# One block of a two-block network on one core: key sums, lora's columns and the second projection's first chain in another order

## What is computed

```python
# first block: one projection for everything, of the context (256 tokens) and x (1024 tokens)
pc = modulate(rmsnorm(ctx, norm1_g), csh1, csc1) @ w_in
px = modulate(rmsnorm(x, norm1_g), sh1, sc1) @ w_in
xr, xk, xv, xw, xa, xgl = split_rwkv(px_rw, shift_mu, grid_shift(px_rw, rows))   # p + mu * (shifted - p)
kk = k * k_k
kk = kk / maximum(sqrt(sum(kk * kk, per head of 64)), 1e-12)
tw = tanh(xw)                                   # then tw @ w_up, xa @ a_up: "lora"
b_x = b_gate * dwconv3(c_gate * u, conv_w)      # short convolution over tokens
x = x + g1 * (concatenate([a_x, b_x]) @ w_out)
...
x = rmsnorm(x, final_g)
# second block
hdn = rmsnorm_2(x, norm_gain)
q_a, k_a, v_a, g_a, q_b, k_b, v_b, g_b = split(hdn @ w_in_2)
q_a, k_a, q_b, k_b = rope(rmsnorm_2(each head, its gain))
mixed = concatenate([o_a * silu(g_a), o_b * silu(g_b)])
x = x + mixed @ w_out_2
```

## Time and profile before

| | us |
|---|---|
| three runs | 2458.22, 2458.24, 2469.73 (median 2458.24) |
| the profiled execution | 2450.08 |
| its span, from first to last instruction | 2448.3 |
| PE busy in the span | 2129.4 (87%) |
| DVE busy | 1654.9 (68%) |
| ACT busy | 1268.3 (52%) |
| POOL busy | 675.0 (28%) |
| mean granted clock of PE | 0.944 of 2.4 GHz |

### The profile page before, as it was taken

One profiled execution on the slowest core, in us unless ns is written; L12 is line 12 of the kernel. 1 busy time (PEld: TensorE's weight loads), 2 busy tenths in 40 slices (PEclk: granted clock), 3 DMA queues, 4 the chain that ended last, 5 costly groups with the idle time before them and its releaser, 6 DMA issues. The chain is left out here.

```text
span 2448.3 us, 50472 instructions
## 1 busy us (share of the span) xinstructions
PE 2129.4 (87%) x21006; PEld 1686.8 (69%) x21006; DVE 1654.9 (68%) x2541; ACT 1268.3 (52%) x2327; POOL 675.0 (28%) x472
## 2 busy tenths in 40 slices
PE   5999998499999988973999999999479899778889
PEld 3777787477888743862788888887367788444567
DVE  3665555698888646236899999997367366477941
ACT  5412121476666654434788888886344443365430
POOL 0000011466666501204123322330254545000011
PEclk8999999699999998986999999999799999898999
DMA  7222233333222167326899999997353643200032
GB/s 273 65 56 72 60 83 70 79 68 68 68 69 69 42 225 267 124 113 234 292 394 385 385 388 395 389 386 266 114 190 112 203 111 95 110 1 1 1 104 78
DMA packets 163488, 398.29 MB, mean 163 GB/s; under 512 B 13231, under 2 KB 57405, under 8 KB 163261
## 3 DMA queue, kind: packets, MB, share of 16 engines
q1 hardware_dynamic: 148220, 345.23, 40.3%
q0 software_dynamic: 12224, 44.57, 6.8%
q10 hardware_dynamic: 2816, 5.26, 0.6%
HBM read 348.35 MB, written 46.66 MB: 161 GB/s over the span
## 5 line engine op out<-in xcount | busy, mean ns | idle before, releaser
L1900 DVE TENSOR_TENSOR exp_w_lo<-exp_w,exp_w_hi 128x2048 fp32r<-128x2048 f32 x186 | 414.4, 2290 | 21.9 <-ACT exp_w_hi L1857 21.7
L1857 ACT ACTIVATE exp_w_hi<-exp_w 128x1024 fp32r<-128x1024 f32 x384 | 377.3, 1052 | 66.9 <-PE bank L1819 51.7
L2091 POOL TENSOR_TENSOR w_lo<-mixT,w_hi 128x512 fp32r<-128x512 f32 (+1 forms) x112 | 153.5, 1395 | 175.7 <-ACT w_hi L2167 173.5
L1819 PE MATMUL bank<-exp_w_hi,xsT_lo 128*128 128x512 f32 x512 | 160.8, 396 | 5.7 <-DVE xsT_lo L1904 5.7
L1819 PE MATMUL bank<-exp_w_lo,xsT_hi 128*128 128x512 f32 x512 | 158.8, 392 | 0.0
L1819 PE MATMUL bank<-exp_w_hi,xsT_hi 128*128 128x512 f32 x512 | 158.5, 391 | 0.0
L1787 POOL DMA_INDIRECT moe_rows<-exp_out,idxT x16 | 25.2, 1572 | 437.8 <-DVE exp_out L1959 437.8
L2151 PE MATMUL bank<-w_hi,h_lo 128*128 128x512 f32 (+1 forms) x320 | 123.4, 386 | 1.1 <-POOL w_lo L2091 1.1
L2151 PE MATMUL bank<-w_lo,h_hi 128*128 128x512 f32 (+1 forms) x320 | 120.7, 377 | 0.0
L2151 PE MATMUL bank<-w_hi,h_hi 128*128 128x512 f32 (+1 forms) x320 | 120.3, 376 | 0.0
L1772 POOL DMA_INDIRECT xs<-xn_rows,idxT x16 | 116.0, 7250 | 14.4 <-DVE idxT L1931 5.7
(11 more groups left out here) (372 smaller groups left out, 5797.3 us busy)
## 6 DMA issues: line engine op xcount, KB each, us to landing
exp_w<-in_exp_w_gate_dram SPq DMA_DIRECT2D x64, 1024.0 KB, 9.9
exp_w<-in_exp_w_up_dram SPq DMA_DIRECT2D x64, 1024.0 KB, 10.6
exp_w<-in_exp_w_down_dram SPq DMA_DIRECT2D x64, 1024.0 KB, 7.5
mixT<-in_w_in_dram SPq DMA_DIRECT2D x96, 256.0 KB, 2.9
ada_w_second<-in_ada_w_dram SPq DMA_DIRECT2D x16, 1024.0 KB, 9.5
chunk<-rkv_scratch SPq DMA_DIRECT2D x80, 192.0 KB, 4.0
w_in_ring<-in_w_in_dram SPq DMA_DIRECT2D x26, 512.0 KB, 3.9
rkv_scratch<-work POOLq DMA_DIRECT2D x16, 640.0 KB, 5.9
```

The source lines that it names most:

```text
L1819: mm = pe.matmul(g.ps[bank + q][:, :], lhs[:, kk, :], wide[:, k, q * 512:(q + 1) * 512], start=(kk == 0 and p == 0), stop=(kk == KT - 1 an ...
L1857: last = act.activation(wh[:, n % RH, k, :], w[:, n % RING, k, :], ACT.Copy)
L1900: dve.tensor_tensor(wl[:, n % RH, :, :], w[:, n % RING, :, :], wh[:, n % RH, :, :], ALU.subtract).then_inc(lo_ok, 1)
L2091: pool.tensor_tensor(wl[:, q % SR, 0:width(q)], w[:, q % WR, 0:width(q)], wh[:, q % SR, 0:width(q)], ALU.subtract).then_inc(w_lo, 1)
```

## The change

It does five things. (1) In the first projection PE makes the head sums not behind the block of `HEADS` but inside it: two parts ahead of k-step 2, the third ahead of k-step 6; DVE takes them ahead of its weight split. (2) The `b`, `c`, `u` blocks of the fourth head move to the end of the list, and 12 comes ahead of 13; ACT does lora's `tanh` in this stage, two blocks behind; the four loads of `lora_up` are issued by SP behind the last weight load, into memory that `g2_row` uses later. (3) In both output stages DVE makes the low part of the first row tile, ahead of its weight splits. (4) In the second projection DVE makes the low part of the weight pieces 1, 3, 5 and 7 of the first block; the chains of rows 0 to 3 are written out in another order; a root of a constant stands first on ACT. (5) The norms of rows 4 to 7 come one product earlier (`START`), at m=7, 9, 19 and 21; their turns and parts stay where they are.

```diff
@@ phase_project
-    for i in range(4):
-
+    for i in range(3):
         order += [("rw", 4 + i), ("b", i), ("c", i), ("u", i)]
-    order += [("rw", j) for j in (8, 9, 10, 11, 1, 2, 3, 13, 12)]
+    order += [("rw", j) for j in (7, 8, 9, 10, 11, 1, 2, 3, 12, 13)]
+    order += [("b", 3), ("c", 3), ("u", 3)]
...
+            for d in range(2):
+                sp.dma_start(g.lora_up[0:64, d, :], g.i["w_lora_up"][0, d]).then_inc(g.up_in, 16)
+                sp.dma_start(g.lora_up[64:128, d, :], g.i["a_lora_up"][0, d]).then_inc(g.up_in, 16)
...
+                if n - 2 == order.index(("rw", 12)):
+                    act.wait_ge(mixed, n - 1)
+                    act.activation(g.lora[0:64, :], g.lora[0:64, :], ACT.Tanh)
...
+                if n in HEADS:
+                    take_key(HEADS.index(n))
                 if n + SR < NT:
                     split_lo(n + SR)
...
+            def key_sums(h, thirds):
+                pe.wait_ge(kcopied, h + 1)
+                for q in thirds:
+                    lo, hi = THIRDS[q]
+                    if 3 * h + q >= 2:
+                        pe.wait_ge(khread, 3 * h + q - 1)
+                    pe.matmul(g.ps[6 + q % 2][:, 0:hi - lo], g.c("head"), ksq[:, lo:hi],
+                              start=True, stop=True).then_inc(khead, 1)
...
+                    if n in HEADS and k in (2, 6):
+                        key_sums(HEADS.index(n), (0, 1) if k == 2 else (2,))
@@ phase_wkv
-            act.activation(g.lora[0:64, :], g.lora[0:64, :], ACT.Tanh).then_inc(tanh_ok, 1)
...
-            pe.wait_ge(up_in, 64)
-            pe.wait_ge(tanh_ok, 1)
+            pe.wait_ge(g.up_in, 64)
             pe.wait_ge(zeroed, 1)
@@ phase_mix_out (phase_second_out alike, with one subtraction)
-            for t in range(TT):
-
+            for t in range(1, TT):
                 pool.wait_ge(m_hi, t + 1)
...
+            dve.wait_ge(m_hi, 1)
+            for k, rows in ((0, g.yT), (4, g.bT)):
+                last = dve.tensor_tensor(ml[:, 0, k:k + 4, :], rows[:, :, 0:P], mh[:, 0, k:k + 4, :], ALU.subtract)
+            last.then_inc(first_lo, 1)
@@ phase_second_project
+    START = {m - 1: t for t, m in AT.items()}
...
             for q, (blk, k) in enumerate(pieces):
+                if q < KT and q % 2:
+                    continue
                 pool.wait_ge(w_hi, q + 1)
...
+            act.activation(rs[:, 0, 0:1], g.c("eps"), ACT.Sqrt).then_inc(chain_a, 1)
+            split(0)
+            root(0, 0)
+            split(1)
+            root(0, 1)
+            root(1, 0)
+            split(2)
+            high(0)
+            split(3)
+            root(1, 1)
...
-                if m in LATER:
-                    root(LATER[m], 0)
-                    root(LATER[m], 1)
+                if m in START:
+                    root(START[m], 0)
+                    root(START[m], 1)
...
             dve.wait_ge(rows_in, 32)
+            final_norm(0)
+            first_low(1)
+            second_norm(0)
+            final_norm(1)
+            first_low(3)
+            low(0)
+            second_norm(1)
...
-                if m in LATER:
-                    final_norm(LATER[m])
-                    second_norm(LATER[m])
+                if m in START:
+                    final_norm(START[m])
+                    second_norm(START[m])
```

More of the change, by code:

```diff
@@ L2627, in _ @@
         def _(dve):
+            dve.wait_ge(m_hi, 1)
+            dve.tensor_tensor(ml[:, 0, :, :], g.mixT[:, :, 0:P], mh[:, 0, :, :], ALU.subtract).then_inc(first_lo, 1)
             for k in range(KT):
```

86 lines of the change are left out of this document (44 added, 42 removed).

## The result

| | before | after |
|---|---|---|
| median of the timed runs | 2461.64 us (4 runs) | 2423.92 us (4 runs) |
| the profiled execution | 2450.08 | 2423.48 |
| its span | 2448.3 | 2421.7 |
| mean granted clock of PE | 0.944 | 0.936 |

The ratio is 0.9856, with a 95% interval of 0.9826 to 0.9887: the changed kernel is 28 to 43 us faster. The forecast was 2428.5, a gain of 29.7. Four more runs, beside 25 of the kernel before (median 2458.07), gave 0.9859 (0.9821 to 0.9896), 34.4 us between the medians.

The account below looks back on a forecast made before the run. PE was taken as the bound, busy 87% of the span, with waits caused by order. The terms sum to 29.7 us, taken off the median 2458.2 to give 2428.5; range 2414 to 2442.

Parts of the forecast that it names:

- key sums: First projection: four PE waits of 2.26 us and two clock falls of 1.55 go; gain 12.1, ends 9.0 and 12.1.
- projection's tail: End of first projection: with a u block last instead of lora, fewer closing operations on DVE and ACT; gain 1.3 us.
- recurrence's start: Earlier lora weights and tanh let PE start 3.5 us sooner, chunk loads late next; gain 3.4, ends 2.5 and 3.5.
- two output stages: DVE makes the first tile's low part, so PE starts sooner; gain 1.0 us each, ends 0 and 1.5 each.
- second projection's start: New order for rows 0 to 3 brings the last turn 2.1 us earlier; gain 2.0, ends -2 and 4.
- later rows: Second projection, rows 4 to 7: earlier norms shorten PE's waits of 13.9 us; gain 8.9, ends 5 and 13.
- four k-steps of products between: First projection: products between k=2 and k=6 let DVE take the sums, so the third finds its bank free.
- Last head's sums and the run of rw blocks: First projection: DVE falls about 7 us behind for one block there, but PE does not notice; cost 0.
- Rival 3: First projection: run of ten rw blocks becomes DVE's, PE waits for splits, slower, 2463 us; chance 0.02.
- its upper end: Recurrence's start: the largest gain allowed for this term, 3.5 us.
- the gain put on DVE's odd pieces: Second projection's start: odd weight pieces ready sooner, closing two PE waits of 1.1 us together.
- the lower end: Second projection's start: DVE's four new subtractions and POOL's may hold each other up; -2 us, total about 26.

Follow-up runs that it names:

- keys_only: Kernel before with only the key sums moved inside the next block and taken ahead of DVE's weight split; median 2441.99 us, ratio 0.9945.
- lora_only: Kernel before with only the new column order, tanh and lora's second weights moved into the first projection; 2451.43 us, ratio 0.9973.
- later_only: Kernel before with only the norms of rows 4 to 7 of the second projection begun one tile earlier; 2442.95 us, ratio 0.9946.
- dve_order: Kernel before with only DVE's order changed, key sums taken ahead of the next weight split; median 2443.44 us, ratio 0.9953.
- again: The changed kernel run once more without any edit; 2414.85, 2416.20, 2431.22 and 2435.34 us.
- pool_pieces: Changed kernel with the low parts of the first block's odd weight pieces back on POOL; one execution, 2411.33 us.
- warm: Changed kernel with seven extra 512-column products at the start of the second attention, same results computed; median 2425.37 us of 4 runs.

## Why the prediction was right, point by point

| term | forecast | measured | from |
|---|---|---|---|
| key sums | 12.1 | 14.1 to 14.5 | keys_only |
| projection's tail | 1.3 | 1.3 | lora_only |
| recurrence's start | 3.4 | 3.3 or 4.3 | lora_only, after |
| two output stages | 1.0 + 1.0 | 1.0 + 1.1 | after |
| second projection's start | 2.0 | 1.1 | after |
| later rows | 8.9 | 10.5 | later_only |
| sum | 29.7 | 32.6 or 33.6 | |

- **Key sums.** The reading that DVE was late only for its place in an order held, and priced alone (dve_order, 12.2 to 12.9) it is the 12.1. What the forecast put at nothing is the sums' place inside the block, 1.6 to 1.9 more. The step "with four k-steps of products between", on which it let the third sum find its bank, was not needed for that: dve_order has no products between and no wait. The reader of the earlier trace rows should have asked what DVE would do if its two steps alone were exchanged: a take of 0.69 us, beside a second sum of 0.94.
- **Last head's sums and the run of rw blocks.** Costed at 0. In after PE has no wait for the sums there; lora_only, with the old sums, has one of 2.96 us, 0.7 more than before. Rival 3 had no place.
- **Recurrence's start.** Right, the chunk's load late next included, but for its upper end: that DVE or POOL may start first, worth 1.0, was not in it.
- **Output stages.** Right in size and releaser. That POOL's low part slowed DVE's splits in the second is borne out by 3.49 us for 6.98.
- **Second projection's start.** Mis-sized by half. Two things held: ACT's first sum of squares at S + 8.5, 2.9 later than before, and the first turn nearly unmoved. The step that failed is the gain put on DVE's odd pieces: they lengthened DVE's chain by 1.2 us, most of it by contention with POOL. That risk had been in the text, as the lower end, and was not in the sum.
- **Later rows.** The waits of the text were 0, 3.0, 1.9 and one behind a low part; measured 0, 2.2, 1.7, 2.9. The term is 1.6 larger: row 5's turn comes 5.8 earlier and not 5.1, since its wait is 0.8 shorter, and from there to row 7's it is 4.7 and not 3.8. PE's clock fell behind row 5's turn in after as it did before; where it stayed up (again, pool_pieces) the term is 1.6 to 2.0 larger still, near the upper end of 13.
- **The sum against profile and median.** Off the median it gave 2428.5 for a measured 2423.9; off the profiled execution 2420.4 for 2423.5. By the profiled pair alone the 29.7 look 3 us too high, although the moved parts gained more: at row 7's turn after was 40.1 ahead, and the attention's clock took 15 of it back in that one execution. That this pair differs by nearly the forecast sum is luck. The medians differ by 34.4 beside 25 runs, near the 32.6 or 33.6 of the parts: the mechanism held, and the sum was 3 to 4 us short.

## What to carry to other kernels

Where a producer waits for a buffer, look first at what the taker's queue holds ahead of the taking, above all a wait for a third engine: exchanging two steps on one queue brought 12.2 to 12.9 of the 14.1 to 14.5 us here. To price a small edit, measure the stretch between two landmarks that enclose it and nothing else: the medians here could not tell 1.6 us, the stretch could. Before comparing two profiles, compare the granted clock stage by stage, since a stage at the edge of it can differ by 15 us between executions of one kernel, more than most edits bring. When starting a chain earlier, check which steps of other chains then stand behind its inner waits.

## What the runs showed of the hardware

- In the attention PE's clock fell to 0.50 and stayed there, for 90 us in after and 130 us in again, while PE was busy for nine tenths or more of nearly every 10 us: at 0.50 a pair's small products (64 rows or 128 columns) take up to 3.45 us instead of 2.76, PE becomes the stage's bound, and 32 pairs of 0.69 more are 22 us (an estimate from these rows), about the spread of the attention, 240 to 259.
- Keeping PE busy for 6.3 us ahead of the stage did not prevent it (warm). One useless product of 256 or 512 columns per pair inside the stage's first half held the clock at full there, and the mean clocks of whole executions are 0.949 to 0.958, beside 0.936 to 0.947 without: adding work made the kernel faster (medians 2399.5 and 2405.7 beside 2412.3).
- The length of a wait does not tell by itself whether the clock falls behind it. In after the turn of eight blocks took 1.94 us behind a wait of 2.94 (row 7), in again 1.06 behind one of 2.95; behind row 5's it took 1.16 in after (2.23) and 1.61 in later_only (2.24). In the kernel before the clock fell behind all four, of 2.80 to 4.30.
- Where a DVE operation with two SBUF inputs and one of POOL fell together, the later one was the longer for it: 2.27 us for 1.28 (DVE's second norm in after), 1.52 for 0.68 (DVE at the recurrence's start in again), 1.54 for 1.04 (POOL there in after).
- The table load in row 5's chain in after took 1.28 us at 1790.92, and the root behind it started at 1792.22. The Trainium skill, ScalarE: Activation LUTs, § What ACT_TABLE_LOAD costs, has 2.66 with a drain, by which, in the prediction's estimate, the later rows would have gained about 4. The trace agrees on the load itself and shows no drain, and they gained 10.5.
